# Building the right rows of the dense gate tiles token by token on VectorE in a mixer and expert kernel on one core

## What is computed

```python
q = (h @ wq).reshape(N, PEER_HEADS, 2, PEER_DHALF)
s = einsum('nhpc,hpkc->nhpk', q, keys)          # 8 heads, 2 lists of 128 scores each
sv, si = top_k(s, 16)
comb = sv[:, :, 0, :, None] + sv[:, :, 1, None, :]
cv, ci = top_k(comb.reshape(N, 8, 256), 16)
expert = i1 * 128 + i2                           # the keys that ci names in the two lists
gate = softmax(cv)
...
a = gelu(einsum('nd,nhkd->nhk', h, u_tab[expert]))
out = einsum('nhk,nhkd->nd', gate * a, v_tab[expert])
```

## Time and profile before

| | us |
|---|---|
| median of 3 runs | 3340.3 |
| lowest and highest | 3336.39, 3342.16 |
| the profiled execution's own time | 3337.24 |
| its span in the profile | 3335.6 |

### The profile page before, as it was taken

How to read it: one execution, slowest core, us unless ns; L and a number is a source line. 1 busy time by engine, 2 the same in 40 slices (tenths; PEclk the granted TensorE clock), 3 DMA queues, 4 the chain that set the end, 5 groups by cost and what they waited for, 6 DMA issues and landing times.

```text
span 3335.6 us, 43974 instructions
## 1 busy us (share of the span) xinstructions
PE 3045.6 (91%) x16658; PEld 2331.2 (70%) x16658; DVE 2407.0 (72%) x4987; ACT 935.2 (28%) x1271; POOL 1489.0 (45%) x1188
## 2 busy tenths in 40 slices
PE   8899978577888469999999999999999999999997
PEld 1466644245555369988888887888888888788886
DVE  1233324999988878887777777878777777778798
ACT  0111111138888622222222222222122222212222
POOL 0010000425554334346656565656565565666453
PEclk9999989889999879999999999999999999999999
DMA  9711131602222367789999999999999999999883
GB/s 357 212 64 63 57 145 64 208 7 108 108 108 108 151 223 264 265 292 353 366 351 366 359 350 368 353 370 353 355 351 369 349 360 344 352 347 336 307 295 140
DMA packets 305919, 858.73 MB, mean 257 GB/s; under 512 B 25376, under 2 KB 108832, under 8 KB 303984
## 3 DMA queue, kind: packets, MB, share of 16 engines
q0 software_dynamic: 151344, 551.09, 45.1%
q1 hardware_dynamic: 154333, 305.79, 25.6%
q10 hardware_dynamic: 108, 0.22, 0.0%
HBM read 793.86 MB, written 63.15 MB: 257 GB/s over the span
## 4 chain that ended last, share of the span: by engine, by line
PE 50%; DMA 5%; POOL 4%; DVE 3%; issue 2%; ACT 0%; DVEq 0%; SPq 0%; ACTq 0%
PE y_ps L1889 22%; PE a_ps L1870 20%; PE picked_ps L1907 5%; DMA shared<-in_peer_u,ids 3%; PE uT_ps L1857 3%; POOL shared L1453 2%; POOL quad L1464 1%; DMA shared<-in_peer_v,ids 1%; DVE uT_lo L1615 1%; DVE shared L1674 1%; DVE shared L1644 0%; DMA quad<-in_peer_v,idsT 0%; DVE shared L1657 0%; ACT uT_hi L1534 0%; DVE m_lo L1630 0%
## 5 line engine op out<-in xcount | busy, mean ns | idle before, releaser
L1453 POOL DMA_INDIRECT shared<-in_peer_u,ids x480 | 560.7, 1168 | 595.3 <-DVE acts L1657 507.1
L1657 DVE CUSTOM_DVE_ANT_0 shared<-shared 128x1024 f32<-128x1024 f32 x480 | 579.2, 1221 | 173.5 <-DMA shared<-in_peer_u,ids 172.9
L1870 PE MATMUL a_ps<-h_hi,uT_lo 128*128 128x320 f32 x2048 | 643.8, 314 | 1.7 <-DVE h_lo L1786 1.7
L1870 PE MATMUL a_ps<-h_hi,uT_hi 128*128 128x320 f32 x2048 | 633.8, 309 | 0.0
L1870 PE MATMUL a_ps<-h_lo,uT_hi 128*128 128x320 f32 x2048 | 633.8, 309 | 0.0
L1889 PE MATMUL y_ps<-v_hi,m_lo 128*128 128x512 f32 x1280 | 511.5, 400 | 25.7 <-DVE shared L1644 14.6
L1644 DVE TENSOR_TENSOR shared<-shared,y_ps 128x512 f32<-128x512 f32 x630 | 422.5, 685 | 150.2 <-PE y_ps L1889 149.5
L1889 PE MATMUL y_ps<-v_lo,m_hi 128*128 128x512 f32 x1280 | 504.6, 394 | 0.0
L1889 PE MATMUL y_ps<-v_hi,m_hi 128*128 128x512 f32 x1280 | 502.3, 392 | 0.0
L1464 POOL DMA_INDIRECT quad<-in_peer_v,idsT x384 | 443.9, 1156 | 120.1 <-issue 120.1
L1870 PEld LDWEIGHTS a_ps<-h_hi,uT_lo 128*128 128x128 f32 x2048 | 386.1, 189 | 7.2 <-issue 2.1
(11 more groups left out here) (187 smaller groups left out, 4197.2 us busy)
## 6 DMA issues: line engine op xcount, KB each, us to landing
shared<-in_peer_u SPq DMA_DIRECT2D x128, 512.0 KB, 7.5
v_all<-in_peer_v SPq DMA_DIRECT2D x128, 512.0 KB, 7.5
gate_blocks<-dense SPq DMA_DIRECT2D x10, 4096.0 KB, 12.1
gates<-gate_blocks SPq DMA_DIRECT2D x64, 640.0 KB, 22.1
w_ada<-in_w_ada SPq DMA_DIRECT2D x12, 2048.0 KB, 11.7
x_in<-in_x_prompt SPq DMA_DIRECT2D x16, 512.0 KB, 4.5
shared<-in_peer_u,ids POOLq DMA_INDIRECT x480, 8.7
shared<-in_w_in SPq DMA_DIRECT2D x8, 768.0 KB, 13.2
```

Source lines behind the costliest of these rows:

```text
L1453: pool.indirect_dma_start(out=rows[n % 4], out_offset=None, in_=u_table if n < DOTS else v_table, in_offset=bass.IndirectOffsetOnAxis(ap=i ...
L1657: nc.vector.tensor_tensor_reduce(out=rows[n % 4], in0=rows[n % 4], in1=token_row, scale=1.0, scalar=0.0, op0=ALU.mult, op1=ALU.add, accum_ ...
L1870: last = nc.tensor.matmul(a_ps[n][:, 0:GROUP], lhs[s][:, k, :], rhs[:, k, tok], start=k == 0 and m == 0, stop=k == KD - 1 and m == 2)
```

## The change

The left rows stay. The right rows are made by DVE alone: for each of the 8 tokens of a batch one `tensor_scalar` compares a row of key numbers (`iota_row`, f32, 128 elements) with the token's right key and multiplies by its gate, both read per partition from columns of `rightT` and `gateT`. It writes `right` directly, so `right_hot` and POOL's `place` go, and DVE waits for the PE matmul that frees `right` (`wait_for_placed`), which POOL did before. `keyT` becomes `leftT` (bf16) and `rightT` (f32), so ACT takes three pieces from `x_ps` rather than two. The sixteen places of `rows` are spread anew, PE turns the slots ahead of `product(prepare, 0)`, ACT takes them ahead of `take_q(prepare, 0)`, and `widen_keys` and the exponential move to later batches.

```diff
 # POOL
-            def place(t):
-                for b in range(BATCHES):
-                    wait_for_placed(pool, d, b)
-                    pool.wait_ge(S.right_hot, d * BATCHES + b + 1)
-                    nc.gpsimd.tensor_tensor(right[b % 2][:, :, :], right_hot[b % 2]..., gateT[...]..., ALU.mult).then_inc(S.right, 1)
...
 # ACT, take_slots
-                nc.scalar.activation(keyT[:, :, :], x_ps[:, 0:2, :], ACT.Copy).then_inc(S.slotsT, 1)
+                nc.scalar.activation(leftT[:, :], x_ps[:, 0, :], ACT.Copy).then_inc(S.slotsT, 1)
+                nc.scalar.activation(rightT[:, :], x_ps[:, 1, :], ACT.Copy).then_inc(S.slotsT, 1)
                 nc.scalar.activation(gateT[:, :], x_ps[:, 2, :], ACT.Copy).then_inc(S.slotsT, 1)
...
 # ACT, period
-                if prepare is not None:
-                    take_q(prepare, 0)
                 if indexed is not None:
                     take_index(indexed)
                 if placed is not None:
                     take_slots(placed)
                 if prepare is not None:
+                    take_q(prepare, 0)
                     take_qT(prepare, 0)
                     take_q(prepare, 1)
...
-                    if choose is not None and b == 6:
+                    if choose is not None and b == 9:
                         widen_keys(choose, 0)
-                    if choose is not None and b == 12:
+                    if choose is not None and b == 14:
                         act.wait_ge(S.shifted, choose + 1)
                         nc.scalar.activation(soft[:, :, :], soft[:, :, :], ACT.Exp).then_inc(S.exp, 1)
-                    if choose is not None and b == 14:
                         widen_keys(choose, 1)
...
 # DVE, hot_rows
                 wait(dve, S.left, d * BATCHES + max(b - 1, 0))
                 nc.vector.tensor_tensor(left_hot[b % 2][:, :, :], leftT[...]..., iota_keys[:, :, :], ALU.is_equal)
-                wait(dve, S.right, d * BATCHES + max(b - 1, 0))
-                nc.vector.tensor_tensor(right_hot[b % 2][:, :, :], key(1), keys_iota, ALU.is_equal)\
-                    .then_inc(S.right_hot, 1)
+                wait_for_placed(dve, d, b)
+                for n in range(BATCH):
+                    t = b * BATCH + n
+                    last = nc.vector.tensor_scalar(right[b % 2][:, n, :], iota_row[:, :], rightT[:, t:t + 1],
+                                                   gateT[:, t:t + 1], ALU.is_equal, ALU.mult)
+                last.then_inc(S.right, 1)
...
 # PE, period
-                if prepare is not None:
-                    product(prepare, 0)
                 if done is not None:
                     turn_slots(done)
                 if prepare is not None:
+                    product(prepare, 0)
                     product(prepare, 1, range(0, 5))
```

More of the change, by code:

```diff
@@ L704, in routing @@
                                "scores_used shifted exp gate_ready keyed slotsT_ps slotsT left_hot left "
-                               "right_hot right place_ps placed out0 out1 best_key key_wide first_keyed dve expert picked row_in used "
+                               "right place_ps placed out0 out1 best_key key_wide first_keyed dve expert picked row_in used "
                                "u0 u1 u2 u3 u4 u5 u6 u7")
@@ L743, in routing @@
         iota_keys = sbuf(nc, mem, "iota_keys", [P, NKEYS, BATCH], BF16)
+        iota_row = sbuf(nc, mem, "iota_row", [P, NKEYS])
         s_ps = psum(nc, mem, "s_ps", [P, HP, NKEYS])
@@ L828, in _ @@
                       allow_small_or_imprecise_dtypes=True).then_inc(S.iota, 1)
+            pool.iota(iota_row[:, :], pattern=[[1, NKEYS]], base=0, channel_multiplier=0,
+                      allow_small_or_imprecise_dtypes=True).then_inc(S.iota, 1)
             def fetch(slot):
@@ L857, in _ @@
                 fetch(slot)
-            periods(period)
         @block.scalar
@@ L886, in take_index @@
                     nc.scalar.activation(idsT[:, ORDER[t], :], x_ps[:, 0, :], ACT.Copy).then_inc(S.slotsT, 1)
-                    nc.scalar.activation(gatesT[:, ORDER[t], :], x_ps[:, 2, :], ACT.Copy).then_inc(S.slotsT, 1)
+                    nc.scalar.activation(gatesT[:, ORDER[t], :], x_ps[:, 2, :], ACT.Copy).then_inc(S.slotsT, 2)
                 else:
-                    act.sem_inc(S.slotsT, 1)
+                    act.sem_inc(S.slotsT, 2)
                     nc.scalar.activation(gatesT[:, ORDER[t], :], slots[:, 2, :, :].rearrange("p h k -> p (h k)"), ACT.Copy)\
@@ L974, in two_lists @@
                     own.mark(nc.vector.max(best[:, n, low], s_ps[:, n, :]))
+                rows(0)
                 own.settle()
@@ L979, in two_lists @@
                     own.mark(nc.vector.match_replace(work3[:, n, :], best[:, n, low], s_ps[:, n, :], NEG))
-                rows(0)
+                    if n % 4 == 3:
+                        rows(1 + n // 4)
                 own.settle()
@@ L984, in two_lists @@
                     own.mark(nc.vector.max(best[:, n, high], work3[:, n, :]))
-                rows(1)
+                rows(5)
                 own.settle()
@@ L989, in two_lists @@
                     own.mark(nc.vector.max_index(best_at[:, n, high], best[:, n, high], work3[:, n, :]))
-                rows(2)
+                    if n % 8 == 7:
+                        rows(6 + n // 8)
                 own.settle()
@@ L1007, in best_pairs @@
                         ALU.add))
-                rows(4)
+                rows(8)
                 own.settle()
@@ L1013, in best_pairs @@
                         own.mark(nc.vector.max(pair[:, h, part], sums[:, h]))
-                    rows(5 + n * 3)
+                    if part is low:
+                        rows(9)
                     own.settle()
@@ L1018, in best_pairs @@
                         own.mark(nc.vector.max_index(pair_at[:, h, part], pair[:, h, part], sums[:, h]))
-                    rows(6 + n * 3)
+                    rows(10 if part is low else 12)
                     own.settle()
@@ L1024, in best_pairs @@
                             own.mark(nc.vector.match_replace(sums[:, h], pair[:, h, low], sums[:, h], NEG))
-                        rows(7)
+                        rows(11)
                         own.settle()
@@ L1124, in rows @@
                     if b == 0 and done is not None:
-                        dve.wait_ge(S.slotsT, done * 2 + 2)
+                        dve.wait_ge(S.slotsT, done * 3 + 3)
                     if placed is not None:
```

33 lines of the change are left out of this document (9 added, 24 removed).

## The result

The changed kernel takes 3379.53 us (median of four runs, 3378.19 to 3386.95) against 3339.44 for the kernel before in the same comparison: 1.0132 times as long, with a 95% interval of 1.0119 to 1.0144. The forecast was 3299, faster; the time lies outside the range.

What follows compares the result with a forecast made beforehand. DVE was taken to bound the placing periods: 40.7 + 9.6 + 25.6 + 1 = 76.9 us against 85.1, so 8.2 saved, five times 41, less 2.5 in period 1: 38.5 off 3337.2, say 3299 us; range 3285 to 3343.

Steps and rivals of the forecast that it cites:

- the price of the `tensor_scalar`: DVE's right rows: 0.20 us each for 128 per tile, 25.6 us; ends 17.7 and 43.5.
- own-load rival (0.27): Right rows on DVE: each scalar has its own load, or one load at one element per step; 3339 us, chance 0.20.
- ACT's chain: ACT per placing period: left rows start after about 8.8 us, then batches, q pieces, widenings, exponential; 75.1 us, below DVE's 76.9.
- the waits on DVE: DVE in `hot_rows`, waiting for matmuls of the batch two before, list operations queued behind: 1 us allowed per period.
- its own list of signs: What would show the forecast right (`tensor_scalar` 0.20 us apart, periods 76 to 78 us) or wrong (0.27 or more, `place_ps` waits).
- the list operations: DVE's list work in each placing period, taken from period 2 and checked by period 1: 40.7 us.
- the left comparisons: DVE's `left_hot`, kept by the change, now always with POOL idle: 16 times 0.60, 9.6 us per period.
- POOL's contention: DVE and POOL hinder each other: `left_hot` takes 2.40 us beside POOL's `right`, 0.60 with POOL idle.
- the rival that it goes: Right rows on DVE: the pair of operations also loses the double rate, 0.34 us each; 3383 us, chance 0.12.
- period 1, charged 2.5: DVE's first two row products come earlier and wait for POOL's fetches: 2.5 us lost, between 0.7 and 4.6.
- the later `widen_keys`: ACT's widenings at later batches only change what stands between batches; two at 1.81 us are in its chain.
- the estimate of 0.127 us: Right rows on DVE by the skill's 58 cycles and half the elements: 16.3 us per tile, no term for the scalars.

Runs made afterwards that it cites:

- e6_left_first: Changed kernel with PE's next first product in the preceding period's last three batches, and two batches' left rows ahead of the second product: 3330.83 us, 0.9985.
- e9_pool_plain: `e7_pool_left_first` with, for periods 0 to 2, row products one place later and the first widening at batch 6 where nothing is placed: 3304.02 us, 0.9902.
- e7_pool_left_first: `e6_left_first` with right rows again compared by DVE in one instruction per batch and multiplied by POOL, as before the change: 3309.84 us, 0.9912.
- e8_one_left_first: `e6_left_first` with the gate left out of the right rows (immediate 1.0), so one per-partition scalar instead of two: 3297.22 us, 0.9879.

## Why the prediction was wrong

**Failed: the price of the `tensor_scalar`.** The text took 0.20 us because "two independent reads can share one" load. They didn't: the measured price is 0.135, 0.195 and 0.256 us for none, one and two scalars. The difference of 0.056 us times 128 is 7.2 us a period, 36 us in all. The own-load rival (0.27) had this price nearly right. It also said that there would be "no waits left to add", and so its 3339 was too low as well.

**Failed: ACT's chain.** The text had `take_q`, `take_qT` and `take_q` "follow sixteen products, 0.44 us each when PE is warm", from 7.03 over 16, and read the same 7.03 us as "two strings of products" where it is one. The 16 in that row counts records; the order listed in the section on the change has `x8` for the same product. The sixteen take 14.4 us (7.09 + 4.56 + 2.74) and, with the turns and waits among them, the left rows come 17.7 us in. The same rows held the warning: ACT's first left rows came 15.8 us after PE's start in the kernel before (798.11 to 813.93), the two products were not shortened by the change, and only the turning of the slots (0.5 us) moved ahead of them. A forecast of 8.8 us had no source for the other 7. (The terms listed for ACT's chain also add up to 74.8, not 75.1; nothing hung on that.)

**Failed with it: the waits on DVE.** With left rows at 8.8 us the text allowed 1 us a period for DVE at `rows(2)`. The two waits make 9.5 (37.1 and 10.2 over 5): 42 us more than allowed. The condition in its own list of signs, "`right` on DVE waiting often for `place_ps`", pointed at the smaller of the two.

**The sum with both mended.** 40.7 + 9.6 + 32.8 (128 times 0.256) + 9.5 = 92.6 us, measured 92.3. From a gain of 38.5, 36 and 42 taken away leave a loss of 40; the medians differ by 40.1. That fit is a little better than the sum deserves, as the 3.5 us that periods 0 and 2 lost are not in it.

**Right:** the list operations at 40.7 and the left comparisons at 0.60 us (`e6_left_first`: 40.7 + 9.6 + 32.8 = 83.1, measured 82.8 with no waits to speak of); that POOL's contention goes; that the double rate stays with a pair of operations, so the rival that it goes fell, and that its time, 3383, was nearest is chance; and period 1, charged 2.5 and found 2.0, with waits for the fetched rows (0.81 and 0.67).

**Not foreseen, small:** the text costed the later `widen_keys` at nothing in the plain periods too. At batch 9 the first widening stands behind ACT's last `take_qT`, and without batches to place ACT comes to that only when PE has made its last product. ACT in order of time, late in period 2 of the changed kernel:

```profile
712.55 0.60 ACT L861 ACTIVATE qT<-x_ps 128x512 f32<-128x512 f32 x1 [0.75 <-PE x_ps L1157]
713.05 1.90 ACT L887 ACTIVATE key_wide<-best_key 128x2048 bf16<-128x2048 bf16 x1
```

DVE then stood for the first widening (1.74 us at 715.05) and for the second (2.04); the kernel before stood for the second alone. Periods 0 and 2 lost 1.9 and 1.6 us, and `e9_pool_plain`, with the widening back at batch 6 there, took 1.8 less in each than `e7_pool_left_first`.

**On the Trainium skill's rule** ("VectorE: DVE Perf Modes", the section on the TRN2 errata): the estimate of 0.127 us from its figure lies close to the 0.135 measured with immediates, and its advice to prefer wide tiles speaks against this change rightly. With two scalars the instruction takes twice that estimate, and the measurement decides.

**Open:** why a scalar costs what it does, which no run shows; and whether a way to apply the gate that costs DVE one scalar and nothing else exists. `e8_one_left_first` shows that it would be worth 8.3 us in five periods over POOL's product (387.02 - 378.72); no such way was tried.

## What to carry to other kernels

Where a chain's start is shortened by reordering, take the measured start of before and subtract what really moved, rather than build it anew from pieces; and count instructions in the order of the program, since records of the trace may be several to one. When work is cut into many small instructions, price one exactly as it will be issued, with all its per-partition scalars. Spreading one engine's work evenly helps only when the engine that takes it over starts as early: mend the late start first, and measure that alone.

## What the runs showed of the hardware

A 128-element f32 `tensor_scalar` pays about 0.06 us on DVE for each per-partition scalar, from 0.135 us with none to 0.256 with two, also when eight stand back to back; a second operation by an immediate cost nothing that shows (0.138 for one operation on uint32). While POOL multiplies, `tensor_tensor` on DVE takes longer, and not in `left_hot` alone: 2048 bf16 elements of `work<-work,key_wide` took 3344 ns on the mean before and 1225 in the change, where POOL is idle. An f32 matmul of 128 by 512 leaves two records on PE, 0.44 us each in the rows above. PE's mean granted clock over the placing periods was 0.96 of full speed before, 0.92 in the change and 0.97 in `e7_pool_left_first`, but the first products of the five placing periods together took no longer in the change (39.0 us) than before (40.1), so the clock does not explain the late left rows.
